# The transposes in the blockwise inversion of RWKV's chunk matrices: by VectorE's turning of 32x32 blocks in place of second TensorE products

## What is computed

```python
def step(S, inp):
    r_t, w_t, k_t, v_t, a_t, b_t = inp
    sa = jnp.einsum('bhvk,bhk->bhv', S, a_t)
    S = S * w_t[:, :, None, :] + sa[..., None] * b_t[:, :, None, :] + v_t[..., None] * k_t[:, :, None, :]
    return S, jnp.einsum('bhvk,bhk->bhv', S, r_t)
xs = (seq_first(r), seq_first(decay), seq_first(k), seq_first(v), seq_first(-kk), seq_first(kk * a))
_, y = lax.scan(step, jnp.zeros((B, H, N, N), f32), xs)
```

## Time and profile before

| | us |
|---|---|
| median of 3 runs | 2379.42 |
| lowest, highest | 2372.02, 2380.36 |
| the profiled execution | 2377.93 |
| its span | 2376.2 |
| TensorE busy | 2183.0 (92%) |
| VectorE busy | 1253.9 (53%) |
| ScalarE busy | 837.1 (35%) |
| GpSimd busy | 319.4 (13%) |

### The profile page before, as it was taken

One profiled execution on the slowest core, in us unless ns is written; L12 is line 12 of the kernel. 1 busy time (PEld: TensorE's weight loads), 2 busy tenths in 40 slices (PEclk: granted clock), 3 DMA queues, 4 the chain that ended last, 5 costly groups with the idle time before them and its releaser, 6 DMA issues. The chain is left out here.

```text
span 2376.2 us, 31528 instructions
## 1 busy us (share of the span) xinstructions
PE 2183.0 (92%) x12916; PEld 1734.4 (73%) x12916; DVE 1253.9 (53%) x1686; ACT 837.1 (35%) x1319; POOL 319.4 (13%) x303
## 2 busy tenths in 40 slices
PE   8999988899999889999899999989995778999997
PEld 6776886788878778887687888866663446878875
DVE  5547764642342566765553453476684445543543
ACT  4344223532242434444342232352224244322322
POOL 0000000200001200000303930234430002000002
PEclk9999998999999999999999999999996769999999
DMA  5120002232222122221122222221100021323221
GB/s 212 63 71 19 3 4 63 80 98 90 97 98 89 62 81 74 77 71 54 62 97 90 93 98 98 98 98 62 54 23 1 1 98 62 116 74 113 98 77 66
DMA packets 50607, 177.17 MB, mean 75 GB/s; under 512 B 5616, under 2 KB 5616, under 8 KB 50208
## 3 DMA queue, kind: packets, MB, share of 16 engines
q1 hardware_dynamic: 46800, 163.86, 21.0%
q10 hardware_dynamic: 3168, 7.60, 0.9%
q0 software_dynamic: 496, 3.69, 0.4%
HBM read 170.94 MB, written 4.19 MB: 74 GB/s over the span
## 5 line engine op out<-in xcount | busy, mean ns | idle before, releaser
L1114 DVE TENSOR_TENSOR w_lo<-w_raw,w_hi 128x1024 fp32r<-128x1024 f32 (+1 forms) x320 | 396.7, 1241 | 811.8 <-ACT w_hi L1107 810.3
L1208 PE MATMUL banks<-xh,w_hi 128*128 128x512 f32 x1560 | 626.7, 402 | 4.3 <-PEq L213 3.6
L1210 PE MATMUL banks<-xh,w_lo 128*128 128x512 f32 x1560 | 611.9, 392 | 0.0
L1209 PE MATMUL banks<-xl,w_hi 128*128 128x512 f32 x1560 | 611.3, 392 | 0.0
L1107 ACT ACTIVATE w_hi<-w_raw 128x1024 fp32r<-128x1024 f32 (+1 forms) x320 | 329.0, 1031 | 800.3 <-PE banks L1210 749.1
L1208 PEld LDWEIGHTS banks<-xh,w_hi 128*128 128x128 f32 x1560 | 295.5, 189 | 87.1 <-issue 20.6
L1210 PEld LDWEIGHTS banks<-xh,w_lo 128*128 128x128 f32 x1560 | 295.0, 189 | 63.7
L1209 PEld LDWEIGHTS banks<-xl,w_hi 128*128 128x128 f32 x1560 | 295.7, 190 | 59.0 <-issue 1.2
L1208 PE MATMUL banks<-hh,w_hi 128*128 128x512 f32 x688 | 270.6, 393 | 11.7 <-DVE w_lo L1114 4.8
L1210 PE MATMUL banks<-hh,w_lo 128*128 128x512 f32 x688 | 269.4, 392 | 0.0
L1209 PE MATMUL banks<-hl,w_hi 128*128 128x512 f32 x688 | 269.2, 391 | 0.0
(11 more groups left out here) (506 smaller groups left out, 2862.4 us busy)
## 6 DMA issues: line engine op xcount, KB each, us to landing
w_raw<-in_w SPq DMA_DIRECT2D x128, 512.0 KB, 3.5
w_raw<-in_w_gu SPq DMA_DIRECT2D x44, 512.0 KB, 3.5
w_raw<-in_w_c_in SPq DMA_DIRECT2D x40, 512.0 KB, 3.5
w_raw<-in_w_ab_in SPq DMA_DIRECT2D x27, 512.0 KB, 3.5
w_raw<-in_w_in SPq DMA_DIRECT2D x25, 512.0 KB, 3.5
w_raw<-in_w_down SPq DMA_DIRECT2D x16, 384.0 KB, 3.0
w_raw<-in_w_down SPq DMA_DIRECT2D x16, 320.0 KB, 2.8
w_raw<-in_w_ab_out SPq DMA_DIRECT2D x8, 512.0 KB, 3.5
```

The lines of the kernel that those rows point to most:

```text
L1114: dve.tensor_tensor(lo[:, 0:n], core.raw[u % RAW][:, 0:n], hi[:, 0:n].bitcast(F32), ALU.subtract).then_inc(core.split_ready, 1)
L1208: pe.matmul(bank, hi[:, w], src.xh[:, kk, :], start=kk == 0, stop=False)
L1209: pe.matmul(bank, hi[:, w], src.xl[:, kk, :], start=False, stop=False)
L1210: mm = pe.matmul(bank, lo[:, w], src.xh[:, kk, :], start=False, stop=last)
```

## The change

The second orientation isn't computed by TensorE any more. VectorE's `transpose` on a tile of 128x512 turns every 32x32 block in its place. Up to level 4 an inverse has entries only in the 32x32 blocks on its diagonal, so turning the blocks transposes it. At level 5, where the 32x32 block off the diagonal appears, only `XT` is computed, by a product with its operands exchanged as before.

- Pairs and masks: the products of line 1550 and `narrow` go. VectorE masks `Nt` first, makes the first `XT` from `Nt` in SBUF, and `X` by one `transpose` of `XT`: 7 operations for each c, in place of 8. VectorE waits only for those of its own results that it reads.
- Levels: the mask is laid on Q (VectorE, into `Q`, in place of ScalarE's copy). TensorE makes 16 products in place of 32 for n = 1 to 16, and 16 as before for n = 17 to 20. VectorE adds them to X straight from PSUM and turns X to XT; at level 5 it adds to XT without turning.
- VectorE's order is: mask Q(n), add the update of n - 1, turn n - 1. TensorE's is Q(n), update of n - 1, as before. Q is in bank 5 or 6, the update in bank 2 or 7. TensorE may begin the levels when `Ark` of c = 2 is masked (12 of 16 masks), before: when all masks are done.
- ScalarE does nothing in the levels.

```diff
             pe.wait_ge(s.q_out, n)
+            if n > 4:
+                pe.wait_ge(s.x_turned, n - 4)
             if n > 2:
-                pe.wait_ge(s.xt_prod, xt_prods(n - 2))
+                pe.wait_ge(s.x_sum, n - 2)
             for i in range(NCH):
                 cols = slice(i * C, (i + 1) * C)
-                if not last:
-                    for e in range(2):
-                        pe.matmul(core.psum[2 + c % 2][half(e), cols], XT[half(e), c, i], Q[half(e), c % 2, i], start=True, stop=True)
                 for e in range(2):
-                    mm = pe.matmul(core.psum[4 + c % 2][half(e), cols], Q[half(e), c % 2, i], XT[half(e), c, i], start=True, stop=True)
+                    q, xt = Q[half(e), c % 2, i], XT[half(e), c, i]
+                    mm = pe.matmul(core.psum[(2, 7)[c % 2]][half(e), cols], q if last else xt, xt if last else q, start=True, stop=True)
             mm.then_inc(s.x_prod, 1)
...
-            for n in range(1, 21):
-                c = (n - 1) % 4
-                bank = core.psum[c % 2].rearrange("p (n t) -> p n t", t=C)
-                act.wait_ge(s.q_ready, n)
-                if n > 2:
-                    act.wait_ge(s.x_prod, n - 2)
-                done(act, act.activation(Q[:, c % 2], bank, ACT.Copy), s.q_out)
...
-                done(dve, dve.tensor_tensor(XT[:, c], bb[:, :, 0:C], lvl("lmask", 0), ALU.mult), s.masked)
...
+                dve.tensor_tensor(Nt[:, c], bb[:, :, 0:C], m(0), ALU.mult).then_inc(s.masked, 1)
+                dve.tensor_tensor(Arb[:, c], bb[:, :, C:P], m(1), ALU.mult).then_inc(s.masked, 1)
+                dve.wait_ge(s.masked, 4 * c + 1)
+                dve.tensor_tensor(XT[:, c], Nt[:, c], lvl("lmask", 0), ALU.mult).then_inc(s.x_first, 1)
+                dve.wait_ge(s.x_first, 3 * c + 1)
+                dve.tensor_tensor(XT[:, c], XT[:, c], lvl("lmask", 6), ALU.add).then_inc(s.x_first, 1)
                 dve.wait_ge(s.k_pairs, c + 1)
...
+                dve.tensor_tensor(Aak[:, c], kb[:, :, 0:C], m(2), ALU.mult).then_inc(s.masked, 1)
+                dve.tensor_tensor(Ark[:, c], kb[:, :, C:P], m(3), ALU.mult).then_inc(s.masked, 1)
+                dve.wait_ge(s.x_first, 3 * c + 2)
+                dve.transpose(rows(X[:, c]), rows(XT[:, c])).then_inc(s.x_first, 1)
+
+            for n in range(1, 22):
+                if n <= 20:
+                    l, c = divmod(n + 3, 4)
+                    view = core.psum[5 + c % 2].rearrange("p (n t) -> p n t", t=C)
+                    dve.wait_ge(s.q_ready, n)
+                    if n > 2:
+                        dve.wait_ge(s.x_prod, n - 2)
+                    dve.tensor_tensor(Q[:, c % 2], view, lvl("lmaskt", l), ALU.mult).then_inc(s.q_out, 1)
+                if n > 1:
+                    c = (n - 2) % 4
+                    view = core.psum[(2, 7)[c % 2]].rearrange("p (n t) -> p n t", t=C)
+                    dve.wait_ge(s.x_prod, n - 1)
+                    if n - 1 <= 16:
+                        dve.tensor_tensor(X[:, c], X[:, c], view, ALU.add).then_inc(s.x_sum, 1)
+                        dve.wait_ge(s.x_sum, n - 1)
+                        dve.transpose(rows(XT[:, c]), rows(X[:, c])).then_inc(s.x_turned, 1)
+                    else:
+                        dve.wait_ge(s.x_turned, n - 5)
+                        dve.tensor_tensor(XT[:, c], XT[:, c], view, ALU.add).then_inc(s.x_sum, 1)
...
-                if c > 1:
-                    pe.wait_ge(s.masked, 6 * (c - 2) + 6)
-                for n in range(NCH):
-                    for e in range(2):
-                        mm = pe.matmul(narrow(c)[half(e), n, :], AR[half(e), c, n, 0, :], bt[half(e), c, n * C:(n + 1) * C], start=True, stop=True)
-                mm.then_inc(s.a_pairs, 1)
...
-            pe.wait_ge(s.masked, 24)
+            pe.wait_ge(s.masked, 12)
```

More of the change, by code:

```diff
@@ L1301, in rwkv @@
         diag = [st.sb(f"diag{i}", [P, NCH, P]) for i in range(2)]
-        prod = [Y[:, 7, :].rearrange("p (n t) -> p n t", t=C), Z[:, 12, :].rearrange("p (n t) -> p n t", t=C)]
         elast = st.sb("elast", [P, 4, NCH])
@@ L1313, in rwkv @@
         Nt, X = chunked(kk), chunked(k)
+        rows = lambda ap: ap.rearrange("p n t -> p (n t)")
         Arb, Aak, Ark = chunked(lw), chunked(a), chunked(r)
@@ L1316, in rwkv @@
         s = st.sems("e_before e_in elast_kept at_ready rt_ready bonus_ready "
-                    "tok tok_out zeroed b_diag k_diag b_pairs a_pairs k_pairs masked x_first "
-                    "q_ready q_out x_prod xt_prod x_next "
+                    "tok tok_out zeroed b_diag k_diag b_pairs k_pairs masked x_first "
+                    "q_ready q_out x_prod x_sum x_turned "
                     "d_ready d_out sa_ready sa_out h_ready h_sum h_out y_ready y_out "
@@ L1324, in wide @@
             return core.banks[:, b:b + 2, :].rearrange("p b (n m) -> p (b n) m", m=P)
-        def narrow(c):
-            return core.psum[(2, 7)[c % 2]].rearrange("p (n t) -> p n t", t=C)
         quarters = lambda bank: bank[:, 0:4 * C].rearrange("p (c t) -> p c t", t=C)
@@ L1333, in tok_bank @@
             return (7, 0, 1, 2, 3, 4, 5, 6)[q % 8]
-        def xt_prods(n):
-            return 2 * n if n <= 16 else 16 + n
         def diagonal(act, to, src, sem):
@@ L1440, in _ @@
                 dve.wait_ge(s.b_pairs, c + 1)
-                done(dve, dve.tensor_tensor(XT[:, c], bb[:, :, 0:C], lvl("lmask", 0), ALU.mult), s.masked)
-                done(dve, dve.tensor_tensor(Arb[:, c], bb[:, :, C:P], m(1), ALU.mult), s.masked)
-                dve.wait_ge(s.a_pairs, c + 1)
-                done(dve, dve.tensor_tensor(Nt[:, c], bb[:, :, 0:C], m(0), ALU.mult), s.masked)
-                dve.wait_ge(s.k_pairs, c + 1)
-                done(dve, dve.tensor_tensor(Aak[:, c], kb[:, :, 0:C], m(2), ALU.mult), s.masked)
@@ L1447, in _ @@
[L1447 to L1465, removed]
@@ L1543, in _ @@
                 if c > 1:
-                    pe.wait_ge(s.masked, 6 * (c - 2) + 5)
+                    pe.wait_ge(s.masked, 4 * (c - 2) + 4)
                 group(diag[0], both, lambda n: wide(2 * c)[:, n, :], s.b_diag, s.b_pairs)
-                if c > 1:
-                    pe.wait_ge(s.masked, 6 * (c - 2) + 6)
-                for n in range(NCH):
-                    for e in range(2):
-                        mm = pe.matmul(narrow(c)[half(e), n, :], AR[half(e), c, n, 0, :], bt[half(e), c, n * C:(n + 1) * C], start=True, stop=True)
-                mm.then_inc(s.a_pairs, 1)
                 if c > 0:
-                    pe.wait_ge(s.masked, 6 * (c - 1) + 3)
+                    pe.wait_ge(s.masked, 4 * (c - 1) + 2)
                 if c == 0:
@@ L1561, in _ @@
                     n += 1
-                    pe.wait_ge(s.x_first, 2 * c + 2)
+                    pe.wait_ge(s.x_first, 3 * c + 3)
                     if l > 1:
-                        pe.wait_ge(s.x_next, 2 * (n - 4))
+                        pe.wait_ge(s.x_sum, n - 4)
                     if n > 2:
@@ L1569, in _ @@
                         for e in range(2):
-                            mm = pe.matmul(core.psum[c % 2][half(e), i * C:(i + 1) * C], Nt[half(e), c, i], X[half(e), c, i], start=True, stop=True)
+                            mm = pe.matmul(core.psum[5 + c % 2][half(e), i * C:(i + 1) * C], Nt[half(e), c, i], X[half(e), c, i], start=True, stop=True)
                     mm.then_inc(s.q_ready, 1)
@@ L1574, in _ @@
             level_products(pe, n, 3)
-            pe.wait_ge(s.x_next, xt_prods(20))
+            pe.wait_ge(s.x_sum, 20)
             def mean(n):
```

## The result

| | before | after |
|---|---|---|
| median, first comparison | 2378.58 us (4 runs) | 2348.57 us (2347.46 to 2355.14, 4 runs) |
| ratio | | 0.9895, interval 0.9877 to 0.9914 |
| median, second chip | 2371.96 us (13 runs) | 2350.24 us (4 runs), ratio 0.9908, 0.9894 to 0.9923 |
| median, third chip | 2372.43 us (11 runs) | 2349.19 us (5 runs), ratio 0.9896, 0.9879 to 0.9913 |
| the profiled execution | 2377.93 us | 2355.14 us, span 2353.4 |

The kernel is 1.0% faster. The forecast was 2357 us, 21.8 us less than before, with a range of 2349 to 2367. The first comparison's medians lie 30.0 us apart and its median of after, 2348.57, is just under the range's lower end; on the two other chips the medians lie 21.7 and 23.2 us apart, and after has 2350.24 and 2349.19.

The account below looks back on a forecast made before the run. VectorE was taken to bound the masks, TensorE the levels. Masks and levels gain 23.8 us, less 2 for the clock: 21.8 off 2377.9 gives 2356.1, set at 2357 us towards the shown median; range 2349 to 2367.

Parts of the forecast that it names:

- What bounds the stage: Before the change VectorE owns the masks and TensorE the levels; after it VectorE takes the stage over, TensorE 95% busy.
- The turning, 0.72 us: VectorE's transpose of a 128x512 fp32 tile, shown in no row, was taken as 0.72 us, by the shuffle's 718 ns.
- The double rate: Rival: the transpose takes 0.49 us or a little less, by the tensor-scalar row; about 2354.5 us, chance 0.08.
- two passes: Rival: fp32 goes through the transpose twice, 1.22 us each, 20 of them 10 us more; 2366 us, chance 0.16.
- block by block: Rival: the transpose works through 16 columns of blocks, 2.7 us each; slower, at 2395 us, chance 0.04.
- Masks, 6.4 us: VectorE's masks were to take 4.41 us per c in place of 5.80, freeing VectorE 6.4 us sooner.
- Pace of the levels, 1.97 us: In the levels each n costs VectorE one mask 0.61, one addition 0.72, one turn 0.64: 1.97 us, before 2.80.
- The hand-offs: Rival: passing between VectorE and TensorE bounds the levels, 16 x 0.32 = 5 us given back; 2362 us, chance 0.10.
- The early start: The last pairs end at 257.1 us and Q(1) and Q(2) follow at once, to 259.0.
- The clock: TensorE idles from 259.0 to 262.6 and its clock falls to half; some 5 us of it lose 2 us.
- Sign (5): In the changed kernel's trace, the recurrence's first product comes near 300.3 us, everything behind it as before, shifted.
- Around the stage: What the clock does behind the levels was worth -1.5 to +1.5 us, centre 0.

Follow-up runs that it names:

- masks_alone: The kernel before with the new masks alone, levels as before: stage 75.1 us against 82.1, ratio to before 0.9973.
- two_turns: The changed kernel with a second turning, into a spare tile, after each of the 16 in the levels: stage 68.2 us, ratio to before 0.9932.
- q_by_act: The changed kernel with Q copied by ScalarE at scale zero and not masked by VectorE (computation incomplete): stage 53.3 us, ratio to before 0.9894.
- late_start: The changed kernel with the levels started when all 16 masks are done, in place of 12: stage 59.2 us, ratio to before 0.9915.
- filled_gap: The changed kernel with 52 more products on TensorE between Q(2) and the update of n = 1: stage 57.0 us, ratio to before 0.9895.
- masks_pool: The changed kernel with Aak and Ark copied by ScalarE and masked in SBUF by GpSimd, not VectorE: stage 58.3 us, ratio to before 0.9893.
- masks_pool_late: masks_pool with GpSimd's 8 masks begun only when Q(3) is masked, inside the levels: stage 54.6 us, ratio to before 0.9881.

## Why the prediction was right, and where it was off

- **What bounds the stage.** Right on both stretches. masks_alone shows VectorE's row of masks on the path, and two_turns that VectorE bounds the levels after the change; TensorE stands 0.05 us an n behind, as q_by_act shows.
- **The turning, 0.72 us.** It is 0.71 in the levels and 0.70 in the masks. The shuffle was the right neighbour and the tensor-scalar row the wrong one. The double rate, two passes and block by block are out. The estimate of 0.71 from "VectorE: DVE Perf Modes", "The three transpose paths", in the Trainium skill holds for fp32 as well.
- **Masks, 6.4 us.** Measured 6.7 on VectorE (24.02 against 17.29), and masks_alone shows 5.8 of it at the first Q. A c takes 4.32, not 4.41: two steps that don't need each other are 0.60 apart, not 0.61, and an operation behind a turning starts 0.62 after it, not 0.64.
- **Pace of the levels, 1.97 us.** Measured 1.92: the addition starts 0.57 behind the mask of Q, not 0.61, and the turn 0.71 behind the addition, not 0.72. Over 16 that is 0.8 us more gain. The hand-offs are hidden, as argued.
- **The early start.** Its place was right (pairs to the end 14.9 us after their start, Q(1) and Q(2) at once), but late_start shows that it carries 0.7 to 1.0 us at most.
- **The clock.** It fell, as counted on, in a wait of 3.28 us. The term was 2 us; filled_gap measures 1.2 to 1.5. This is the step that was mis-sized, by its length: the prediction counted some 5 us of work at the half clock, and TensorE worked there for 2.8 us. With 0.8 from the pace, 0.3 from the masks and 0.6 from here, 21.8 becomes 23.5, and the stage gained 23.9. Sign (5), the recurrence's first product near 300.3, leaves these 2 us out, unlike the sum. It came at 301.29, with the pairs begun 1.07 later than before: 300.2 on the prediction's scale, some 2 us ahead of what the sum implies.
- **Around the stage.** Taken as zero, with bounds of 1.5 us for the recurrence. The first pair of profiles has +1.28 in the recurrence, but the changed kernel's own three have 62.8, 61.3 and 62.5 us, at a granted clock of 0.87, 0.91 and 0.88. Over all twelve profiled kernels it took from 60.2 us at 0.96 (filled_gap) to 63.5 at 0.87 (masks_alone_2), with the same instructions. So up to 3 us of the differences between whole executions lie in this stretch, with its clock, and they follow no edit in particular; where the rest of the scatter lies isn't shown.
- **The level.** I put the forecast between the profiled execution and a median of three runs. That median was some 7 us above those of 9, 11 and 13 runs of the same kernel on other chips (2371.88, 2372.43, 2371.96). The range had 8 us below the forecast for it, and the first median of after lay 0.4 us outside. What failed is the base: three runs from 2372.02 to 2380.36 do not fix a median to 1.5 us.

## What to carry to other kernels

Price a new operation on VectorE by the neighbour that moves data in the same way (here the shuffle), and add up starts, not durations: what an operation waits for decides its step, 0.60 or 0.71 us here. When work moves from one engine to another, ask what is queued ahead of it there: the mask of Q cost little in the pace, but its place behind the masks of c = 3 cost 3.5 us at the start. Work that only a later step needs can go to an idle engine, if that engine is kept away from the operations that it disturbs.

## What the runs showed of the hardware

- GpSimd's fp32 operation on two SBUF tiles beside a VectorE operation with both inputs in SBUF stretched the latter from 0.69 to between 0.82 and 1.65 us (masks_pool), and left those with one input in PSUM (0.65 to 0.69) and the turning (0.71) alone. The Trainium skill, "VectorE: DVE Perf Modes", "Two Vector instructions with no wait between them", says that the second of two SBUF inputs is read through an interface shared with GpSimd; these runs agree with it.
- A wait for the operation ahead costs VectorE 0.11 to 0.13 us each: steps of 0.725 us with it in the masks of before, of 0.60 without it in the change, and of 0.71 for the one operation there that waits for the one just ahead. The same page of the Trainium skill, "The DRAIN you can't avoid", says that a semaphore after each operation costs nothing extra in a row of copies. That isn't at odds with these runs: in both kernels every operation raises a semaphore, and only the wait for it differs.
- TensorE's granted clock fell to the 1.2 GHz level in the wait of 3.28 us, and stayed at 2.4 GHz through the wait of 0.23 us in masks_pool_late and the filled gap. In masks_pool it fell at about 264.0, behind a wait of 2.39 us that had ended at 263.76: a fall can come after TensorE has gone back to work.
